# Sixteen attention units moved from the delta stage to the retention stage, with page issues and semaphore clears moved

## What is computed

```python
h  = _rmsnorm(x, lp['norm_pre'])
pr = _split_proj(h @ lp['w_in'])
ro, ret_new = _retention(rq, rk, heads(pr['ret_v']), ret_state)          # 4 heads
o_cmp, o_sel, o_win, win_new = nsa_fn(q, _rope(q, pos), rows, win_rows, pos)
no = gate[:, :, 0] * o_cmp + gate[:, :, 1] * o_sel + gate[:, :, 2] * o_win   # 8 heads
go, gdn_new, conv_new = _gated_delta(...)                                # 4 heads
mix = jnp.concatenate([ro, no, go], axis=-1)
y   = x + _rmsnorm(mix @ lp['w_out'], lp['norm_post'])
```

## Time and profile before

| | us |
|---|---|
| median of 3 executions | 2279.68 (2278.21 to 2285.9) |
| the profiled execution | 2280.29 |
| its span, first to last instruction | 2278.70 |
| project, layer one | 0 to 292.5 |
| retention | 294.2 to 358.6 |
| delta | 359.7 to 632.0, next stage from 646.8 |
| sample attention | 646.8 to 1055.2 |
| out_project | 1059.1 to 1139.3 |

### The profile page before, as it was taken

How to read it: one execution, slowest core, us unless ns; L and a number is a source line. 1 busy time by engine, 2 the same in 40 slices (tenths; PEclk the granted TensorE clock), 3 DMA queues, 4 the chain that set the end, 5 groups by cost and what they waited for, 6 DMA issues and landing times. The chain is left out here.

```text
span 2278.7 us, 34709 instructions
## 1 busy us (share of the span) xinstructions
PE 1985.9 (87%) x11560; PEld 1354.8 (59%) x11560; DVE 982.7 (43%) x2408; ACT 813.6 (36%) x1894; POOL 512.9 (23%) x806
## 2 busy tenths in 40 slices
PE   6999957989968999996879999689898599999967
PEld 3644446778846676664336444567787467767633
DVE  2154355555533543443222542655654344444322
ACT  2211102334435655551222111033344366556502
POOL 0110011223243434420001100112232443444100
PEclk9999967999979999997989999689999799999979
DMA  5443111000068978853044520200000778888331
GB/s 190 157 162 118 37 41 25 1 11 1 5 162 185 211 169 205 197 131 125 0 161 149 198 80 28 51 16 1 11 1 21 182 185 181 198 208 197 92 125 42
DMA packets 173050, 242.55 MB, mean 106 GB/s; under 512 B 50714, under 2 KB 132282, under 8 KB 172192
## 3 DMA queue, kind: packets, MB, share of 16 engines
q1 hardware_dynamic: 143328, 146.81, 25.1%
q0 software_dynamic: 29536, 93.43, 15.6%
HBM read 223.23 MB, written 25.50 MB: 109 GB/s over the span
## 5 line engine op out<-in xcount | busy, mean ns | idle before, releaser
L611 PE MATMUL bank<-W,hT 128*128 128x512 f32 (+3 forms) x1152 | 444.4, 536 | 14.1 <-DMA W<-in_w_in 8.9
L611 PEld LDWEIGHTS bank<-W,hT 128*128 128x128 f32 x1152 | 213.9, 192 | 202.5 <-issue 173.3
L988 PE MATMUL bank<-XT,W 128*128 128x256 f32 (+1 forms) x768 | 246.9, 459 | 0.0
L1045 POOL DMA_DIRECT2D PS<-in_cache_nsa_kv x256 | 151.0, 590 | 270.4 <-issue 237.8
L1045 POOL DMA_DIRECT2D SHARED<-in_cache_nsa_kv x256 | 151.6, 592 | 184.5 <-DVE RP L958 103.3
L1273 ACT ACTIVATE Pr<-bank,mx 128x31 f32<-128x31 f32 (+4 forms) x192 | 85.7, 447 | 283.0 <-DVE mx L1461 282.8
L988 PEld LDWEIGHTS bank<-XT,W 128*128 128x128 f32 x768 | 136.0, 190 | 67.7 <-issue 50.4
L970 PE MATMUL bank<-CF,RP 128*128 128x128 f32 x1024 | 149.8, 295 | 24.2 <-DVE RP L958 24.0
L977 ACT ACTIVATE XT<-bank 128x512 f32<-128x512 f32 x256 | 141.1, 601 | 40.5 <-PE bank L970 40.4
L970 PEld LDWEIGHTS bank<-CF,RP 128*128 128x128 f32 x1024 | 126.6, 152 | 32.2 <-DVE RP L958 27.6
L1240 POOL TENSOR_TENSOR work<-UP,SHARED 128x512 f32<-128x512 f32 x56 | 72.9, 1307 | 249.0 <-DVE UP L1532 137.3
(11 more groups left out here) (426 smaller groups left out, 3470.8 us busy)
## 6 DMA issues: line engine op xcount, KB each, us to landing
SHARED<-in_cache_nsa_kv SPq DMA_DIRECT2D x256, 128.0 KB, 5.5
SHARED<-in_cache_nsa_kv POOLq DMA_DIRECT2D x256, 128.0 KB, 5.2
PS<-in_cache_nsa_kv SPq DMA_DIRECT2D x256, 128.0 KB, 5.5
PS<-in_cache_nsa_kv POOLq DMA_DIRECT2D x256, 128.0 KB, 5.0
W<-in_w_in SPq DMA_DIRECT2D x48, 512.0 KB, 3.7
XS<-scratch_conv_p POOLq DMA_DIRECT2D x24, 384.0 KB, 4.5
PW<-in_state_nsa_win SPq DMA_DIRECT2D x16, 512.0 KB, 3.8
Wo<-in_w_out SPq DMA_DIRECT2D x4, 2048.0 KB, 12.1
```

The source lines that it names most:

```text
L611: return nc.tensor.matmul(bk((c * NTILE + t) % BANKS)[:, 0:b - a], hT[:, k, t * P:(t + 1) * P], W[:, k // 2, k % 2, 0:b - a], start=(k == ...
L988: mm = nc_(self.v).tensor.matmul(out, self.v['W1'][:, kv, s, :], seg[:, s], start=(s == 0), stop=(s == SEG // PAIRS - 1))
L1045: e.dma_start(where[side * HD:(side + 1) * HD, slot, :, :], A['cache_nsa_kv'][l, page].rearrange("(p r) a g d -> p r (a g d)", r=PAIRS)[:, ...
```

## The change

Three things are changed.

1. `clear` sorts a stage's semaphores by number and clears each run of neighbours with one instruction; it is used in `stage` and after the sample stage.
2. The code of a unit moves into a class, `Attend`, that both stages use. Retention now takes the 16 units of tile 3 for the branches of selected blocks and window (8 heads by 2 branches, 512 keys each), in groups of 4 units with one merge each; the merge has three POOL operations. Retention's steps become a list of 29, `STEPS`: the front is "turn" and "att", the four updates of the sampled state are steps of their own in one bank (`SU`) after tile 2's back, the value product `VM` is made in two halves, and the compression's steps are "rows", "halves", "silu" and "second". Units stand between them at an even pace. The query and value products of the sampled tile are put in columns of U that hold raw queries, and 11 more semaphores make 20.
3. Delta has 80 units left: of tile 3 the 8 compressed ones, whose merge adds to what is in MIX; the tiles of the units come as 2, 0, 3, 1 in place of 3, 0, 1, 2. The delta rule's tiles come as 4, 0, 1, 2, 3 in place of 0, 4, 1, 2, 3. POOL's `first_pages` stands right after the step ("norm1", 3).

```diff
+def clear(nc, sems):
+
+    numbers = sorted(s.num for s in sems)
+    first = numbers[0]
+    for a, b in zip(numbers, numbers[1:] + [None]):
+        if b != a + 1:
+            nc.gpsimd.sem_clear(range(first, a + 1))
+            first = b
...
-            for s in got:
-                nc.gpsimd.sem_clear(s)
+            clear(nc, got)
             nc.all_engine_barrier()
...
-    ORDER = [("front", 0), ("front", 1)]
-    for i in range(NTILE):
-        ORDER += [("back", i)] + ([("front", i + 2)] if i + 2 < NTILE else []) + [("norm", i)]
-    ORDER = [(what, i, TILES[i]) for what, i in ORDER]
+    STEPS = [("turn", 0), ("att", 0), ("turn", 1), ("att", 1), ("back", 0), ("turn", 2), ("att", 2), ("norm", 0), ("rows", 0), ("back", 1), ("turn", 3),
+             ("att", 3), ("norm", 1), ("back", 2), ("state", 0), ("state", 1), ("norm", 2), ("state", 2), ("state", 3), ("turn", 4), ("att", 4),
+             ("back", 3), ("norm", 3), ("halves", 0), ("halves", 1), ("back", 4), ("silu", 0), ("norm", 4), ("second", 0)]
+    heads = Attend.groups_of(EARLY_TILE, (1, 2), False)
+    NU = sum(len(g[1]) * len(g[2]) for g in heads)
+    ORDER, u = [("unit", 0), ("unit", 1)], 2
+    for j, step in enumerate(STEPS):
+        ORDER.append(step)
+        while u < NU and u < (NU + 1) * (j + 1) / len(STEPS) + 1:
+            ORDER.append(("unit", u))
+            u += 1
+    ORDER += [("unit", k) for k in range(u, NU + Attend.BACK)]
...
+                if what == "rows":
+                    dve.wait(e, f"att1{TILES[2]}")
+                    for k in range(2):
+                        cps[0].transposes(e, pe, act, dve, k)
...
+                if what == "state":
+                    q, hp = divmod(i, 2)
+                    dve.wait(e, f"ss{i-1}m" if i else f"s1{TILES[1]}")
+                    if hp == 0:
+                        dve.wait(e, f"vm{q}")
+                    for k in range(2):
+                        mm = nc.tensor.matmul(bk(SU, 4)[:, 2 * k:2 * k + 2, :], KDc_[0:64, 0, hp * P:(hp + 1) * P], VM[k][:, :, hp * P:(hp + 1) * P],
                                               start=True, stop=True)
-                pe.done(e, f"su{t}", mm)
-                beside(what, i)
+                    pe.done(e, f"sv{i}", mm)
...
+EARLY_TILE = 3
+JOINT_TILES = (2, 0, 3, 1)
...
-    TILES = (0, 4, 1, 2, 3)
+    TILES = (4, 0, 1, 2, 3)
...
-    beside = {0: ready(4), 4: state(0) + ready(1), 1: sampled + ready(2), 2: state(1) + ready(3), 3: state(2)}
-    DELTA = ready(0)
+    beside = {4: ready(0), 0: sampled + ready(1), 1: state(0) + ready(2), 2: state(1) + ready(3), 3: state(2)}
+    DELTA = ready(4)
...
-                if what == "unit" and x >= BACK and (x - BACK) % GROUP == GROUP - 1:
-                    merge((x - BACK) // GROUP)
-            dve.wait(e, "n33")
-            first_pages(e, A, l, v, 1)
+                if (what, x) == ("norm1", 3):
+                    dve.wait(e, "n33")
+                    first_pages(e, A, l, v, 1)
+                if what == "unit":
+                    attend.pool_unit(e, x)
...
-    for s in pc_rows[0] + pc_rows[1] + sel_rows[0] + sel_rows[1] + [win_rows]:
-        nc.gpsimd.sem_clear(s)
+    clear(nc, pc_rows[0] + pc_rows[1] + sel_rows[0] + sel_rows[1] + [win_rows])
```

## The result

The changed kernel takes 2293.26 us (median of 20 executions, 2277.98 to 2310.98), the kernel before 2282.11 (20 executions beside them, 2272.58 to 2291.29). The ratio is 1.0059, with a 95% interval from 1.0041 to 1.0078. Forecast were 2245 us and a range of 2206 to 2271. The profiled execution of the changed kernel took 2306.16 us, 13 above that median; its span is 2304.6. A ratio leaves out executions of more than 1.5% above the fastest of their kernel, here two of e4's ten.

The account below looks back on a forecast made before the run. The kernel was taken as bound by TensorE's matmuls while the clock is full. Per layer -31.5 + 27.9 - 9.3 - 4.5 = -17.4 us, two layers -34.8, from 2280.29 to 2245 us; range 2206 to 2271.

Parts of the forecast that it names:

- Clears and tail: Stage borders and delta's end: 4.5 us a layer from clears in runs, 9.3 from earlier page issues.
- the 3.0 us: Border after delta: time taken as POOL's handling of page issues behind their spans, gone if done beside PE.
- cost no instruction of note: Said of the new units' buffers and the sampled tile's products in raw q columns; priced at nothing.
- Units into retention: Retention: 64.8 us of PE work at full clock plus four waits, together 92.3, so 27.9 longer a layer.
- the two named waits: Retention: PE waits for DVE at the cache rows' turn, 5.0 us, and at the third state step, 4.2.
- half clock after those waits: Retention: some 8 us of PE work behind the waits at 1/0.59 in place of 1, priced 5.5 us.
- Units out of delta: Delta: 16 units fewer, 37.8 us, less 4.5 for bared joints and 1.8 for clock, saves 31.5 a layer.
- a lower clock after these waits: Delta: clock loss behind the bared joints, 1.8 us a layer, 0.7% of the window.
- the 4.5: Delta: nine more joints with under 1 us of units, at 0.5 us each, 4.5 us a layer.
- The one that ended on the right side: Delta is a chain, its joints bared: slower if under 14.1 us a layer saved; up to 2308; chance 0.08.
- Retention doesn't take them in: Retention: DVE's minima delay the chain of tiles, so all 37.8 us add; 2265 us; chance 0.13.
- The rival of the pages: Delta's end: POOL's page issues and DVE's work disturb each other, 5.1 us a layer; 2256 us; chance 0.02.

Follow-up runs that it names:

- e4: Changed kernel with 24 idle transposes added on TensorE in each of retention's two long waits: 2273.36 us.
- e1: Kernel before with only clears in runs and POOL's page issues right behind norm1 of tile 3: 2251.74 us, ratio 0.9862.
- e5: e1 with the delta rule's tiles in the new order 4, 0, 1, 2, 3: 2223.9 us, ratio 0.9758.
- e9: e2 with the units' tiles in the old order 3, 0, 1, 2 in place of 2, 0, 3, 1: 2248.44 us.
- e2: Changed kernel with all 96 units back in delta and none in retention: 2286.06 us, ratio 1.0025.
- e3: Changed kernel with the delta rule's tiles in the old order 0, 4, 1, 2, 3: 2299.0 us.
- e8: Changed kernel with retention's list reordered, ACT's copy ahead of the exponential, and the delta rule's tiles in the old order 0, 4, 1, 2, 3: 2268.02 us.
- e14: Changed kernel with retention's list reordered, ACT's copy ahead of the exponential, and delta's 80 units by tiles 2, 0, 1, 3: 2258.19 us.
- e6: Changed kernel with retention's list reordered against its two long waits, same work on every engine: 2258.9 us, ratio 0.9907.
- e15: e14 with the units' tiles as 2, 1, 0, 3 and two idle transposes on PE in each of delta's 80 units: 2264.81 us.

## Why the prediction was wrong

From before to after one edit at a time, by the medians of the whole kernel:

| step | us | difference |
|---|---|---|
| before, beside e1 | 2280.0 | |
| clears in runs, early pages (e1) | 2251.7 | -28.3 |
| tiles 4, 0, 1, 2, 3 (e5) | 2223.9 | -27.8 |
| new retention list and shared class, no units moved (e9) | 2248.4 | +24.5 |
| units' tiles 2, 0, 3, 1 in place of 3, 0, 1, 2 (e2) | 2286.1 | +37.6 |
| 16 units moved (after) | 2293.3 | +7.2 |

Each median is good to some 3 us (the kernel before went from 2278.3 to 2282.1 from round to round), and the table is one path: the tile order gave 28 us here, and 6 and 11 where the units were fewer and in another order (e3, e8).

The step that failed is the clock. The sum let the filled retention and the thinned delta run near the full clock, with 5.5 and 1.8 us a layer for the rest, and the lower level cost some 20 and 28. Beside that, three edits of the bundle (the tile order, the order of the units, the new list) stood at nothing in the sum.

- **Clears and tail: right.** 27.6 us forecast, 28.3 measured; the tail is 4.68 us, 5.5 forecast, so the 3.0 us did go with POOL's issues. The traces name them: DRAIN, which stands on POOL between a stage's last work and the clears, takes 3.37 us right behind the issues, and 0.72 in the changed kernel, where merges lie between.
- **Tile order: costed at nothing, and it is worth 14 us a layer in the old unit order.** I looked only at what it adds. It takes the sampled tile's state away from a stretch where DVE was busy for 20.9 of 30 us and the units small.
- **Order of the units: left out of the sum.** The diff shows it in one line, and I priced the number of units in a joint, not which. It is the largest loss, 19 us a layer.
- **New list of retention: "cost no instruction of note", 12 us a layer.** PE's work at full clock is the same, PE's idle time grows by 4 us (24.3, before 19.9) and its clock is lower (0.57, before 0.61). Whether the four state steps or the cut fronts do it stays open.
- **Units into retention: 92.3 us forecast, 103.2 measured** (to the last merge, as forecast; 100.97 to PE's last instruction). PE's work at full clock was right: 85.06 x 0.77 = 65.5, forecast 64.8. So were the two named waits, 4.50 and 4.66 where 5.0 and 4.2 stood. Idle PE is 15.9 us. What failed is the last term, half clock after those waits: 5.5 us forecast, 85.06 - 65.5 = 19.6 measured. One wait of 4.66 us was followed by 18.7 us at half clock, and nothing in the sum let a wait cost more than its like in work. The premise under it, that the stage's clock is low "because it waits so much" and filling the waits gives it back, didn't fit either: PE was busy for 6.44 of 10 us at 0.50 and for 5.75 at 0.98.
- **Units out of delta: 31.5 us forecast, 11.3 measured.** Again the clock: idle PE was to be 33 us and is 27.4, but PE's busy time, forecast 205.7, is 233.5. My 1.8 us for "a lower clock after these waits" is 28 with this order of units. Against e2, where only the 16 units differ, delta saves 20.6: idle PE grows by 5.7 us, near the 4.5, but PE's busy time falls by 26.2 in place of 37.8, so there the 1.8 is 11.6. In the good order the same 16 units still give back little: e14's delta is 247.6 where e9's is 261.9 and 256.1, some 11 us for 37.8 us of work.
- **The rivals.** The one that ended on the right side said that bare joints would take delta's saving. Its price was near (delta saved 11.3 where it put the break-even at 14.1), but by luck: PE's idle time in delta is 27.4 us and was 28.6, and what grew is the time at the lower clock. The number of thin joints doesn't set that clock. Counted as in the forecast, e2's order has 12 of 61 joints with under 1 us of units and runs at 0.89; the order of e5 and e9 has 13 and runs at 0.94 to 0.97.
- "Retention doesn't take them in" put 37.8 us more on retention, and 38.4 were measured. Its mechanism is out by e6, where the same units in another list leave 89.7 and 85.4 us.
- The rival of the pages is out: eight issues take 5.10 us, 0.64 each, as before, though beside three of DVE's minima only. The Trainium skill's figure of 3100 ns is for an issue beside a DVE copy ("SBUF — State Buffer", "A bandwidth-pool intuition that's wrong (but worth ruling out)"). It isn't seen in this case: 82 of POOL's issues overlap a copy of cache rows (L958) in the trace of the kernel before, and the longest of them takes 0.75 us.

The Trainium skill has the mechanism that I should have made a rival: "TensorE: Matmul & The Clock Gate", in "A second HAM failure mode: psum-queue depth-cycling", tells of a kernel whose PE rests shortly between groups of matmuls, and whose clock swings between its two levels for that. e2 and e9 agree as far as they go: the same matmuls, 21.7 and 17.6 us of rest, 0.89 and 0.94.

## What to carry to other kernels

Where small steps and filler work share TensorE, price a change of order by the clock as well: read which stretches stand at the lower level, what rested ahead of them, and count all work of such a stretch at that level, not only the rest itself. Taking filler out of a stage that runs near full clock can give back much less than its own time (here 11 of 37.8 us). Look at a stage's borders too: here a low clock at the end of one stage went on for 25 us of the next. Try the edits of a bundle one by one: on this path two of these five gained 56 us together, and the other three lost 69.

## What the hardware showed

- The granted clock stayed at 0.50 for 16.0 us of the changed kernel (376.29 to 392.30) and for 14.3 us of e15 (625.37 to 639.63) while PE was busy without a gap, so a full engine didn't get its clock back at once. Behind the wait of 4.50 us it was back within 5.
- The same program at the same place can fall on either side: retention of e4 took 102.89 and 92.59 us in its two layers, delta of e3 260.65 and 249.92. The executions of the changed kernel spread over 33 us, those of before over 19; that more stretches near that edge make the wider spread is my reading and not shown.
- Transposes that nothing reads kept the clock up: with 24 of them in retention's first wait (1.79 us of rest left of 4.50) the next matmuls took 1.09 us in both layers of e4, and 1.94 in the changed kernel.
- One clear of a range of semaphores costs far less than its single ones: before, single clears follow one another every 0.071 us, and the range of the 17 ahead of retention takes 0.135. That border went from 5.53 to 4.49 us of idle PE.
- POOL's DRAIN right behind eight page issues ended 2.8 us after the last of them; with merges between, the issues cost the border nothing that shows (4.68 us in place of 14.92).
